# Hybrid decoder step: the sample group's state turns, late stores and VectorE's order in the front, and the sums of squares in w_out

## What is computed

```python
def decoder_layer(h, ...):
    xn = rmsnorm(h, g_mix)
    z, xbc, dt_raw, q, k, v = split(xn @ w_in)
    y_ssd, new_conv, new_ssm = ssd_branch(z, xbc, dt_raw, conv_prev, ssm_prev, ...)
    y_att = sink_attention(q, k, v, bias, mask, sinks)   # sample: 128 cached keys and the new ones
    h = h + concat(y_ssd, y_att) @ w_out
    h = h + cross_attention(rmsnorm(h, g_cross), mem_k, mem_v, w_cq, w_co)
    h = h + (silu(hn @ w_gate) * (hn @ w_up)) @ w_down    # hn = rmsnorm(h, g_ffn)

def ssd_branch(...):
    conv = silu(causal conv of width 4 over [conv_prev, xbc]); xs, B, C = split(conv)
    dt = softplus(dt_raw + dt_bias); A = -exp(a_log)
    y, new_ssm = ssd_scan(xs, dt, A, B, C, ssm_prev)      # y_off = C @ old state, y_diag inside the chunk
    y = gated_group_rmsnorm(y + d_skip * xs, z, g_norm)
```

## Time and profile before

| what | value |
|---|---|
| median of 3 runs | 2922.1 us (2920.59 to 2925.93) |
| the profiled execution's own time | 2920.1 us |
| its span | 2918.3 us |
| TensorE busy | 2784.7 us, 95% |
| VectorE busy | 1456.0 us, 50% |
| ScalarE busy | 1167.6 us, 40% |
| GpSimd busy | 1007.9 us, 35% |
| mean granted TensorE clock | 0.975 |

### The profile page before, as it was taken

The page is one execution under the profiler, slowest core; times in us unless marked ns, Lnnn a source line. Parts: engine busy times, 40 slices in busy tenths (PEclk is TensorE's granted clock), DMA queues, the critical chain, the costliest instruction groups (busy, mean ns, idle before and its releaser), DMA issues. The chain is left out here.

```text
span 2918.3 us, 34707 instructions
## 1 busy us (share of the span) xinstructions
PE 2784.7 (95%) x13539; PEld 2249.1 (77%) x13539; DVE 1456.0 (50%) x2193; ACT 1167.6 (40%) x1878; POOL 1007.9 (35%) x451
## 2 busy tenths in 40 slices
PE   6889789999999999999999999999999987999998
PEld 3468667878778878878778878888778876888886
DVE  3445565556662285557652475556742445321224
ACT  3345644543452244443452345443542333322222
POOL 1123114333334433433334433333344432333331
PEclk8889989999999999999999999999999999999998
DMA  9554454322223354222223343222223341222221
GB/s 306 190 141 128 140 152 126 87 84 72 73 77 97 100 167 108 80 83 72 78 75 101 109 149 104 80 87 73 73 86 95 120 131 44 79 81 83 83 80 59
DMA packets 415094, 303.05 MB, mean 104 GB/s; under 512 B 48075, under 2 KB 384079, under 8 KB 413890
## 3 DMA queue, kind: packets, MB, share of 16 engines
q1 hardware_dynamic: 412474, 294.41, 33.6%
q10 hardware_dynamic: 1880, 6.34, 0.6%
q0 software_dynamic: 576, 0.07, 0.0%
HBM read 277.90 MB, written 23.85 MB: 103 GB/s over the span
## 5 line engine op out<-in xcount | busy, mean ns | idle before, releaser
L1620 POOL TENSOR_TENSOR w_lo<-w_raw,w_hi 128x1024 fp32r<-128x1024 f32 x398 | 975.7, 2455 | 1748.6 <-ACT w_hi L1634 1748.6
L1634 ACT ACTIVATE w_hi<-w_raw 128x1024 fp32r<-128x1024 f32 x398 | 419.3, 1054 | 553.7 <-PE G L2926 270.5
L2612 PE MATMUL L<-xa_h,w_hi 128*128 128x512 f32 x1184 | 474.9, 401 | 0.0
L2613 PE MATMUL L<-xa_h,w_lo 128*128 128x512 f32 x1184 | 464.1, 392 | 0.0
L2614 PE MATMUL L<-xa_l,w_hi 128*128 128x512 f32 x1184 | 463.5, 391 | 0.0
L2612 PEld LDWEIGHTS L<-xa_h,w_hi 128*128 128x128 f32 x1184 | 223.9, 189 | 54.0 <-issue 6.7
L2614 PEld LDWEIGHTS L<-xa_l,w_hi 128*128 128x128 f32 x1184 | 223.8, 189 | 48.3
L2613 PEld LDWEIGHTS L<-xa_h,w_lo 128*128 128x128 f32 x1184 | 224.1, 189 | 45.9 <-issue 1.0
L2612 PE MATMUL L<-xb_h,w_hi 128*128 128x512 f32 x576 | 231.2, 401 | 14.2 <-DVE xb_l L2041 14.2
L2614 PE MATMUL L<-xb_l,w_hi 128*128 128x512 f32 x576 | 225.5, 391 | 0.0
L2613 PE MATMUL L<-xb_h,w_lo 128*128 128x512 f32 x576 | 225.4, 391 | 0.0
(11 more groups left out here) (570 smaller groups left out, 4939.7 us busy)
## 6 DMA issues: line engine op xcount, KB each, us to landing
w_raw<-in_w_down_dram SPq DMA_DIRECT2D x88, 512.0 KB, 3.5
w_raw<-in_w_gate_dram SPq DMA_DIRECT2D x66, 512.0 KB, 3.8
w_raw<-in_w_up_dram SPq DMA_DIRECT2D x66, 512.0 KB, 3.8
w_raw<-in_w_in_dram SPq DMA_DIRECT2D x56, 512.0 KB, 3.8
xt<-xT_dram SPq DMA_DIRECT2D x56, 256.0 KB, 4.0
w_raw<-in_w_gate_dram SPq DMA_DIRECT2D x44, 256.0 KB, 2.8
w_raw<-in_w_up_dram SPq DMA_DIRECT2D x44, 256.0 KB, 3.1
fwin<-in_w_in_dram SPq DMA_DIRECT2D x8, 1156.0 KB, 10.2
```

The costliest lines, as they stand in the source:

```text
L1620: pool.tensor_tensor(w_lo[:, n % RING, 0:w], w_raw[:, n % RING, 0:w], w_hi[:, n % RING, 0:w].bitcast(F32), ALU.subtract)\
L1634: act.activation(w_hi[:, n % RING, 0:w], w_raw[:, n % RING, 0:w], ACT.Copy)\
L2612: pe.matmul(acc, wh, rh, start=(k == 0), stop=False)
L2613: pe.matmul(acc, wl, rh, start=False, stop=False)
```

## The change

In the front:

- TensorE turns the states of seven sequences right behind the attention scores, and the eighth behind the turned x, B and C. The decay product `diff` and the turned probabilities move back, the latter behind `yoff` and `yd`.
- ScalarE copies six of them ahead of the SiLU of the convolution, the seventh behind it, the eighth behind the decays' exponentials.
- VectorE makes 1+e (`dt_u`) ahead of the convolution instead of behind it, and so waits there for ScalarE's exponential (`dt_e`).
- SyncE issues the two copies of old cache rows to the outputs behind the first panels instead of ahead of the prompt's first block, and three more of the state stores ahead of the wait for `x_sb`.

In stage W the sum of squares of tile i-1 stands ahead of the first norm's part for the last two tiles too, in all four blocks.

```diff
@@ SyncE
-                for src, dst in ((cache_swa_k, s_swa_k), (cache_swa_v, s_swa_v)):
-                    sp.dma_start(dst[0, :, 0:WIN - TS]..., src[0, :, TS:WIN]...).then_inc(early["late_out"], 16)
                 sp.wait_ge(f["wq"], 1)
...
+                for src, dst in ((cache_swa_k, s_swa_k), (cache_swa_v, s_swa_v)):
+                    sp.dma_start(dst[0, :, 0:WIN - TS]..., src[0, :, TS:WIN]...).then_inc(early["late_out"], 16)
...
+                for n in range(2, 5):
+                    state_out(n)
                 sp.wait_ge(f["x_sb"], 3)
                 sp.dma_start(xs_dram.ap(), x3[:].rearrange("p k t -> p (k t)")).then_inc(early["hs_out"], 16)
-                for n in range(2, NB):
+                for n in range(5, NB):
                     state_out(n)
@@ ScalarE
                 act.activation(zt[:], G[S:P, 0, :], ACT.Silu).then_inc(f["ze"], 1)
+                def states_in(a, z):
+                    for bb in range(a, z):
+                        act.wait_ge(f["st_t"], bb + 1)
+                        act.activation(stT[:, bb, :], L[:, bb % 2, :], ACT.Copy).then_inc(f["st_sb"], 1)
+                states_in(0, 6)
                 act.wait_ge(f["conv"], 1)
                 act.activation(xbcS[:], convS[:], ACT.Silu).then_inc(f["xbc"], 1)
+                states_in(6, 7)
...
+                states_in(7, NB)
                 act.wait_ge(f["diff"], 1)
@@ VectorE, front
+                dve.wait_ge(f["dt_e"], 1)
+                dve.tensor_scalar(u, e, 1.0, None, ALU.add).then_inc(f["dt_u"], 1)
                 dve.wait_ge(f["raw"], 1)
...
                 last.then_inc(f["conv"], 1)
-                dve.wait_ge(f["dt_e"], 1)
-                dve.tensor_scalar(u, e, 1.0, None, ALU.add).then_inc(f["dt_u"], 1)
@@ TensorE
                 last.then_inc(f["sc"], 1)
+                pe.wait_ge(f["st_in"], 16 * NB)
+                pe.wait_ge(f["raw"], 1)
+                states_in(0, 7)
                 pe.wait_ge(f["da"], 1)
...
-                pe.wait_ge(f["rda"], 1)
-                pe.matmul(G[0:S, 2, :], gtS[:], rdaS[:], start=True, stop=True).then_inc(f["diff"], 1)
                 pe.wait_ge(f["ze"], 1)
                 pe.wait_ge(f["xbc"], 1)
@@ VectorE, stage W
-                            if i >= 1 and n < KT - 2:
+                            if i >= 1:
                                 sum_squares(b, 0, i - 1)
...
-                        if n >= KT - 2:
-                            sum_squares(b, 0, n - 1)
```

More of the change, by code:

```diff
@@ L770, in _ @@
                 act.activation(stat[:, 5, :], stat[:, 3, :], ACT.Exp).then_inc(f["prob"], 1)
-                for bb in range(NB):
-                    act.wait_ge(f["st_t"], bb + 1)
-                    act.activation(stT[:, bb, :], L[:, bb % 2, :], ACT.Copy).then_inc(f["st_sb"], 1)
                 act.wait_ge(f["pt"], 1)
@@ L1118, in _, with states_in @@
                 last.then_inc(f["sc"], 1)
+                def states_in(a, z):
+                    for bb in range(a, z):
+                        if bb >= 2:
+                            pe.wait_ge(f["st_sb"], bb - 1)
+                        for i in range(4):
+                            last = pe.transpose(L[:, bb % 2, i * P:i * P + P], stN[:, bb, i, :], ident[:])
+                        last.then_inc(f["st_t"], 1)
+                pe.wait_ge(f["st_in"], 16 * NB)
+                pe.wait_ge(f["raw"], 1)
+                states_in(0, 7)
                 pe.wait_ge(f["da"], 1)
@@ L1135, in _ @@
                 last.then_inc(f["xtok"], 1)
[L1136 to L1151 removed]
+                states_in(7, NB)
+                pe.wait_ge(f["rda"], 1)
+                pe.matmul(G[0:S, 2, :], gtS[:], rdaS[:], start=True, stop=True).then_inc(f["diff"], 1)
                 pe.wait_ge(f["st_sb"], NB)
@@ L1163, in _ @@
                 last.then_inc(f["yd"], 1)
+                pe.wait_ge(f["pn"], 1)
+                pe.wait_ge(f["bt_sb"], 1)
+                pe.wait_ge(f["ex"], 1)
+                for bp in range(4):
+                    pe.transpose(G[:, 1, bp * P:bp * P + P], sS[:, bp, 0:WIN], ident[:])
+                for bp in range(4):
+                    last = pe.transpose(G[0:S, 5, bp * P:bp * P + P], sS[:, bp, WIN:], ident[:])
+                last.then_inc(f["pt"], 1)
                 pe.wait_ge(f["pt_sb"], 1)
```

20 lines of the change are left out of this document (2 added, 18 removed).

## The result

Before: 2921.35 us (median of 4 runs, 2918.08 to 2925.93). After: 2903.06 us (4 runs, 2902.70 to 2905.87), ratio 0.9932, 95% interval [0.9917, 0.9947]. That is 18.3 us less; forecast were 10.6 with a range down to 2906. The direction was right, the size was too small.

What follows compares the result with a forecast made beforehand. TensorE, busy 95%, bounds the main phase, so only its waits count; a four-piece VectorE, first-block and SyncE chain bounds the front. Front 6.8 plus stage W 4.1 made 10.9, rounded to 10.6: 2911.5 us median, range 2906 to 2919.

Steps and rivals of the forecast that it cites:

- SyncE's two moves: Front: cache copies moved behind the panels, 2.8 us at the first block; three state stores moved ahead, 1.1 us.
- the engines' 2.9 us: Front: earlier w_out and GpSimd decays shorten Bz, residual at 82.2 instead of 85.20, 2.9 us gained, 0 to 3.9.
- dt_u and the states in TensorE's wait: Front: convolution 2.1 us later, but 28 of 32 state turns fit TensorE's wait; w_out 3.9 us earlier, at 72.1.
- Bz: Front, VectorE: still starts at 79.56 but ends at 82.2, GpSimd's decays being over by 80.3; residual gains 2.9 us.
- The prompt's first block: Front, cross attention: squares bound by ScalarE, not landing; row norms at 113.3 instead of 118.98, 5.7 us, 2.8 from the block.
- SyncE's end: End of front: one store behind ScalarE's last copy, SyncE ending 0.8 us after it instead of 2.0; 1.1 us more.
- Stage W, blocks 1 to 3: Sums moved ahead: 0.7 us each in blocks 1 and 2 (0 to 2), 2.75 us in block 3.
- Stage W, block 0: The sum moves into an idle stretch and TensorE doesn't wait for it: 0, with 1 us either way.
- A: Rival: front gains only the cache copies' and SyncE's part, mix no sooner, Bz stays at 85.2; about 2915; chance 0.13.
- B: Rival: stage W gives nothing, late first norm and clock eat block 3's gain; 6.8 us gained, 2915.3; chance 0.12.
- C: Rival: first block lands no sooner, bound by the queue; Bz and stage W give little; 2919; chance 0.08.
- D: Rival: slower, main phase's first loads wait for late stores; landing at 162 gives 2929; chance 0.05.

Runs made afterwards that it cites:

- SyncE alone: Only SyncE's order changed (cache copies behind the panels, three state stores ahead of the x copy's wait) against the kernel before: 2913.4 us, ratio 0.9975.
- sums alone: Only the sums of squares in stage W moved, front as in the kernel before: 2914.7 us against 2920.0, ratio 0.9976.

## Why the prediction was too small

Two terms of its sum failed. Block 0 of stage W stood in it with nothing, because "TensorE doesn't wait for it", and was worth 2.3 us. And SyncE's two moves stood in it with 2.8 and 1.1 us and gave 6.8, while the engines' 2.9 us were 1.7. Two more things had no term: TensorE's clock 52 us into the main phase (1.3 us) and ahead of the end (0.9). Point by point, as measured over the traces:

- **dt_u and the states in TensorE's wait**: the mechanism was right, the size a little large. w_out came 3.7 us earlier in the first trace (forecast 3.9), and counted from the exponential of dt it is 3.1 over ten traces (28.7 against 31.8). In the first trace two misses met: `yoff` started at 58.73 instead of the forecast 59.9, but took 5.03 us instead of 3.7 by the clock. That they cancel is luck.
- **Bz**: right in mechanism (GpSimd), and 3.3 us for the residual against 2.9 in the first trace, again from two misses: `Bz` started 1.4 us before the 79.56 of the forecast, and took 3.8 us where the forecast had 2.6. Counted from the exponential the residual came 2.5 us earlier. `Bz` took 2.2 us in the ten traces in which the decays did not run beside it, and 3.0 to 4.2 in six with the states turned early in which they did. Not seen: the memory keys' copies on ScalarE stand in the norm. In the first trace of after the root was done at 87.75 and ScalarE's scaling came at 89.04, behind the copies, and w_cq comes 0 to 1.5 us later behind the residual than it did. That takes 0.8 of the 2.5, and leaves the engines' 1.7.
- **The prompt's first block**: 6.3 us to the row norms against 5.7 in the first trace, 5.4 on average behind the exponential. Of this SyncE alone gives 3.5, where the forecast had 2.8, and the engines 1.7, where it had 2.9. TensorE's wait of 2.78 us is the 2.8; the rest, w_cq's product in 5.3 us instead of 6.3, goes by the clock and is not the change's: it took 5.1 to 6.6 us in kernels of both kinds.
- **The clock at the end of the front**: missing. I removed TensorE's wait of 2.78 us and did not price the slow passes behind it: 0.6 us for eight turns in the first trace. ScalarE's last copy came 1.9 us nearer to the row norms there (27.3 to 25.4), and 1.4 in SyncE alone.
- **SyncE's end**: 1.1 us forecast, 1.6 measured, and 1.5 more went with it by the clock 52 us into the main phase.
- **Stage W, blocks 1 to 3**: 0.7, 0.7 and 2.75 forecast; 0.7, 0.7 and 2.75 to 3.3 measured, and 0.9 more behind block 3. That the 0.7 fit is partly luck: it was a choice between 0 and 2, and the single traces spread more than that.
- **Stage W, block 0**: "TensorE doesn't wait for it: 0, with 1 either way" was wrong. TensorE waited 3.2 us for `xb_l` right behind that sum in the trace of before, and I had not read the wait that follows the moved operation.

In sum: 8.4 for the front, 1.3 for the clock behind it (1.5, in thirteen of fifteen), 2.3, 0.7, 0.7 and 3.3 in stage W and 0.9 at the end make 17.6 us. All other stretches of the main phase are the same within 0.3 us in all traces. The medians differ by 18.3 and 19.4, the latter with a ratio's interval from 16 to 23 us; the 0.7 to 1.8 us left are within that, and stay open. Of the rivals, A is refuted by `Bz` and w_out, B (stage W gives nothing) by the 5.3 us of the sums alone, C by the squares that wait for no landing. D, the late stores, too: the first load goes out 3.4 us behind ScalarE's last copy in every trace with three stores ahead, and 5.0 to 5.9 in those without.

## What to carry to other kernels

When a wait of TensorE is removed, look at the granted clock of the passes behind it: here eight took 1.65 us behind the wait and 1.04 without it, a gain on top of the wait's. When an operation is moved, read the next wait of the bounding engine behind its new place, even if it waits for something else; here, on two engines of which one holds the other, 0.1 us decided which of two later operations was held. And compare stages between two events of a trace: by absolute times the engines' moves seemed to give nothing at the row norms, counted from an event of the front they gave 1.7 us alone and 1.9 on top of SyncE's.

## What the runs showed of the hardware

- Beside GpSimd's decays, which start 1.00 us apart, VectorE's two-input operations of 64x1 took 0.92 to 0.94 us instead of 0.15 and started 1.00 us apart too: one for each decay. `Bz`'s operations of 64x256 took 1.12 us instead of 0.34 beside decays 1.05 us apart. So the price is per operation and not per element, and small operations pay the most for their size. The Trainium skill ("SBUF — State Buffer", Who interferes with whom) calls the port pair an exclusive lock; these rows agree for operations with two SBUF inputs, and the residual with one PSUM input took its 0.68 us beside the decays. So did three TENSOR_SCALAR of 64x1, at 0.15.
- After one and the same wait of 1.97 us the granted clock fell in seven traces and stayed in thirteen, all with the same program for 52 us ahead of it. After another of 1.93 us, close to the end, it stayed up in five of twenty. No row shows what decides it.
- VectorE came past its wait for `Bz`'s stores at 77.4 to 80.6 us with the same SyncE order ahead of them in all kernels, and the exponential of dt came at 41.2 to 45.6: the front moves by 4 us from one execution to the next from its first loads on, so absolute times of two traces are not compared below that, and stages between two events are.
